# Sharing the first row scaling of a second RMS norm between VectorE and ScalarE, and moving the wait for the sub-keys, in a one-core Trainium2 decoder block

## The chip, the cores and the metric

The kernel runs on one core of one Trainium2 chip. A core has the engines TensorE (PE in the profile, its weight loads PEld), VectorE (DVE), ScalarE (ACT), GpSimd (POOL) and SyncE (SP, which issues the DMAs here). The metric is the device time of one execution in microseconds (us), lower is better. The kernel before takes 3376.47 us, the median of 3 runs (3375.99 to 3376.52).

## The reference, cut to what matters

One layer of a hybrid decoder trunk over 16 meta tokens and 512 real tokens of width 2048:

```python
h = h + concat([att, rec]) @ w_out          # attention and a recurrent mixer
h = h[:, N_META:]                            # 512 tokens x 2048
h = h + peer_ffn(rms_norm(h, ln_ffn_g), peer_w_q, peer_sub_keys, peer_u, peer_v)
```

The change lies at the start of the second line's work. `rms_norm` divides each token's row by the root of its mean square and multiplies by a gain per column. `peer_ffn` then multiplies the normed rows by `w_q` (8 heads x 256 columns), splits each head's query into two halves, scores each half against 128 sub-keys, and picks the 16 best experts out of 128 x 128 by the two halves' top 16. All products are in float32, kept accurate by splitting both operands into a high and a low part and adding three products.

## The kernel before, in words

Everything is one program of successive stages, each with its own block of instructions per engine: `project`, `attend`, `recur`, `mix_out` (the product with `w_out`), `route` (second norm, query product, scores, top 16), `gate_table`, `experts`. An engine's instructions run in the order in which they are written; between engines there are only semaphores (a wait stands ahead of an instruction, an increment behind one). `route` starts at about 920 us of the trace and ends at about 1175 us, `experts` runs from about 1325 us to the end.

Tokens lie as four tiles of 128 rows (`TB` = 4), the 2048 columns as 16 columns of 128 (`DC` = 16). At the start of `route`:

- VectorE finishes the statistics and the inverse root (`inverse_root`, lines 104 to 108), then `scale_row` (line 1863) multiplies h by it, tile by tile and half a row (1024 columns) at a time, into `scaled_rows`. The four first halves stand ahead of everything; the four second halves stand between the first four `low_column` instructions.
- TensorE keeps itself busy with three products on the identity, then `turn_x` (line 1611) transposes the scaled rows, 4 transposes (one for each tile) per column, into one of four PSUM banks. The first four columns are turned ahead of the first product, later ones one per column of the first head.
- ScalarE's `high_column` (line 1688) takes a turned column out of PSUM, times the gain, as the high part; VectorE's `low_column` (line 1868) makes the low part.
- TensorE's `head(0, ...)` multiplies column by column: 6 matmuls (3 products for 2 query halves), each column after its `x_low`. Ahead of head 0 stands `pe.wait_ge(keys_loaded, 16)`: the sub-keys, a load of 1 MB that SyncE issues at the start of `route` (line 2614, behind the 1 MB load of the gain row). They are first used in `scores(1, ...)` (line 1622), after the first quarter of head 1's product, which scores head 0.
- GpSimd's `plain` (line 2622) waits for all eight half rows, multiplies the last tile by the gain row, and SyncE stores it (line 2617) ahead of the loads of `w_q` for head 1. Behind `plain` GpSimd makes the low parts of `w_q` (`split_low`, line 179).

The order around the change is written out by hand; there is no planner.

```python
            stay_busy_with(pe, q_bank[1][1][:, :].rearrange("p (b t) -> p b t", t=P), cst["ident"], 3)
            for c in range(len(turn_banks)):
                turn_x(c)
            pe.wait_ge(keys_loaded, 16)
            each_head(pe, head, 4)
```

Of the kernel before, what the change touches and what calls it, by code (L numbers as in the profile page):

```python
# [25 lines left out]
ACT = mybir.ActivationFunctionType  # L26
# [7 lines left out]
D = 2048  # L34
DC = D // P
T = 512
TB = T // P
# [1462 lines left out]
def early_step(key, half):  # L1500

    return PH + key // 2, key % 2 * 2 + half
# [7 lines left out]
NORM_HALVES = 2  # L1510


def route(nc, place, kb, stream, h, scaled_rows, sums, xT, picks, cst, load_keys, keys_loaded, plain, plain_stored,
# [3 lines left out]
    with ExitStack() as ctx:  # L1517
        def sem(name):
            return ctx.enter_context(nc.semaphore(f"route_{name}"))
# [15 lines left out]
        stat = place("route_norm_stat", [P, 4, TB], F32, kb)  # L1535
        x_hi, x_lo = xT
        gain = cst["ln_ffn"]
        meaned, rooted, scaled = sem("meaned"), sem("rooted"), sem("scaled")
        x_turned, x_high, x_low = sem("x_turned"), sem("x_high"), sem("x_low")

        q_done, q_out, s_done, s_out = sem("q_done"), sem("q_out"), sem("s_done"), sem("s_out")
# [18 lines left out]
        @block.sync  # L1560
        def _(sp):
            load_keys(sp)
            stream.load_rest(sp, PH)
            for key in range(EARLY + LATER // 2):
                for half in range(2):
                    load_early_half(sp, stream, u, key, half)

        @block.gpsimd
        def _(pool):
            def weigh(m, s, cs=range(2)):  # L1570

                if 0 in cs:
                    pool.wait_ge(places_met, m - 1)
                for c in cs:
                    last = pool.tensor_tensor(
                        hot[:, s, c], hot[:, s, c],
                        idx_f[:, s, c].unsqueeze(2).to_broadcast([P, TB, TOPK, TOPK]), ALU.mult)
                if 1 in cs:
                    last.then_inc(hot_done, 1)

            def head(m, s, first):
                for g in range(QSTEPS):
                    if not (first and m == 0 and g < 2):
                        stream.split_low(pool, m, g)
                    if g == 1 and not first:
                        weigh(m, s)

            plain(pool, scaled, NORM_HALVES * TB)
            each_head(pool, head, 2)
            stream.split_low_in_pieces(pool, *early_step(0, 0))  # L1590
            stream.split_low_in_pieces(pool, *early_step(0, 1))
            stream.split_low_in_pieces(pool, *early_step(1, 0))
            weigh(PH, 0, [0])
            stream.split_low_in_pieces(pool, *early_step(1, 1))
            weigh(PH, 0, [1])
            stream.split_low_in_pieces(pool, *early_step(2, 0))
            stream.split_low_in_pieces(pool, *early_step(2, 1))
            stream.split_low_in_pieces(pool, *early_step(3, 0))
            stream.split_low_in_pieces(pool, *early_step(3, 1))
            stream.split_low_in_pieces(pool, *early_step(EARLY, 0))  # L1600

        @block.tensor
        def _(pe):
            stream.start_free(pe)

            def turn_x(c):
                if c >= len(turn_banks):
                    pe.wait_ge(x_low, c - len(turn_banks) + 1)
                for tb in range(TB):
                    pe.wait_ge(scaled, c // (DC // NORM_HALVES) * TB + (tb + 1))  # L1610
                    last = pe.transpose(turn_banks[c % len(turn_banks)][:, tb, :],
                                        scaled_rows[:, tb, c * P:(c + 1) * P], cst["ident"][:, :])
                last.then_inc(x_turned, 1)

            def scores(m, s, wait_bank=True):

                for k in range(2):
                    pe.wait_ge(q_out, m * 2 + (k - 1))
                    if wait_bank:
                        pe.wait_ge(s_out, m * 2 + (k - 5))  # L1620
                    for tb in range(TB):
                        last = pe.matmul(s_bank[s][k][:, tb, :], qT[:, k, tb * P:(tb + 1) * P],
                                         cst["sub_keys"][:, m * 2 + (k - 2), :],
                                         start=True, stop=True)
                    last.then_inc(s_done, 1)
# [42 lines left out]
            stay_busy_with(pe, q_bank[1][1][:, :].rearrange("p (b t) -> p b t", t=P), cst["ident"], 3)  # L1668
            for c in range(len(turn_banks)):
                turn_x(c)  # L1670
            pe.wait_ge(keys_loaded, 16)
            each_head(pe, head, 4)
            for key in range(EARLY):
                early_key(key)
# [2 lines left out]
        def _(act):  # L1677
# [13 lines left out]
            def split_rows():  # L1691
                act.wait_ge(meaned, 1)
                act.activation(stat[:, 2], stat[:, 1], ACT.Sqrt).then_inc(rooted, 1)
                for c in range(DC):
                    high_column(c)
                    if c % QSPAN == QSPAN - 1 and c >= 2 * QSPAN - 1:
                        stream.split_high(act, *divmod(c // QSPAN + 1, QSTEPS))
# [45 lines left out]
        def _(dve):  # L1743
# [128 lines left out]
            dve.tensor_scalar(stat[:, 1], stat[:, 0], 1.0 / D, EPS, ALU.mult, ALU.add).then_inc(meaned, 1)  # L1872
            dve.wait_ge(rooted, 1)
            inverse_root(dve, link, *(stat[:, k] for k in (3, 1, 2, 0)))
            for tb in range(TB):
                scale_row(0, tb)
            for c in range(DC):
                if c < TB:
# [846 lines left out]
```

## Time and profile before

| | |
|---|---|
| median of 3 runs | 3376.47 us (3375.99 to 3376.52) |
| the profiled execution's own time | 3382.86 us |
| its span, first to last instruction | 3380.8 us |
| PE busy | 3301.9 us (98% of the span) |
| DVE busy | 2184.1 us (65%) |
| ACT busy | 1115.2 us (33%) |
| POOL busy | 1184.8 us (35%) |
| mean granted clock of TensorE | 0.996 |

The span is that of the one profiled execution, which took 6.39 us longer than the median of the runs. Busy shares are averages over stages with different limits. A start in the timeline is in us from the span's first instruction, a row with a count (x5) covers instructions that follow each other, and what stands in brackets is the idle time ahead of it and what ended it. Matmuls overlap, so the busy time of single ones adds up to more than the time they take together.

### The profile page before, as it was taken

The page shows a single profiled execution, that of the slowest core. Times are in us where ns is not written, and L with a number is a line of the kernel's source. Part 1 is how long each engine was busy: PE and PEld are TensorE (multiplying, and loading weights), DVE is VectorE, ACT ScalarE, POOL GpSimd, SP SyncE. Part 2 cuts the span into 40 slices and gives each one's busy share as a digit, 9 for nine tenths or more (in the row PEclk, how much of TensorE's full clock was granted, in tenths as well). Part 3 has the DMA queues.
Part 4 walks back from the last instruction along what each step waited for, and adds up shares of the span by engine and source line. Part 5 has one row for each costly group of instructions (what it writes and reads, how often), then busy time and mean ns, then how long its engine had stood idle before and what let it go on. Part 6 is the DMA issues. An engine that isn't in the chain of part 4 may idle for free.

```text
span 3380.8 us, 49648 instructions
## 1 busy us (share of the span) xinstructions
PE 3301.9 (98%) x16960; PEld 2897.7 (86%) x16960; DVE 2184.1 (65%) x3841; ACT 1115.2 (33%) x1746; POOL 1184.8 (35%) x914
## 2 busy tenths in 40 slices
PE   8999999999999889999999999999999999999999
PEld 6778877878787788889989998999899899989988
DVE  2003413881168898787877677777777777777776
ACT  3122223652232397332222223222222223222321
POOL 3344431454345501243433223322333333333332
PEclk9999999999999999999999999999999999999999
DMA  4233330004332256888888888888888888888886
GB/s 151 81 89 97 94 87 26 26 26 143 105 100 83 93 201 233 270 288 302 300 297 272 267 265 262 274 265 267 262 270 266 264 271 264 265 262 271 267 263 233
DMA packets 369233, 686.52 MB, mean 203 GB/s; under 512 B 212816, under 2 KB 213200, under 8 KB 365904
## 3 DMA queue, kind: packets, MB, share of 16 engines
q1 hardware_dynamic: 295408, 416.79, 39.0%
q0 software_dynamic: 73728, 268.47, 23.2%
q8 instruction: 57, 0.93, 0.1%
q14 instruction: 40, 0.33, 0.0%
HBM read 654.76 MB, written 30.41 MB: 203 GB/s over the span
## 4 chain that ended last, share of the span: by engine, by line
PE 61%; DVE 0%; issue 0%
PE shared L2273 10%; PE shared L2271 10%; PE shared L2272 10%; PE exp_o L2295 7%; PE exp_o L2297 7%; PE exp_o L2293 7%; PE shared L2293 3%; PE shared L2295 3%; PE shared L2297 3%; PE exp_o L241 0%; DVE h L2418 0%
## 5 line engine op out<-in xcount | busy, mean ns | idle before, releaser
L2273 PE MATMUL shared<-x_high,exp_ul 128*128 128x384 f32 x1920 | 641.7, 334 | 0.0
L2271 PE MATMUL shared<-x_high,exp_uh 128*128 128x384 f32 x1920 | 641.6, 334 | 0.0
L2272 PE MATMUL shared<-x_low,exp_uh 128*128 128x384 f32 x1920 | 641.5, 334 | 0.0
L2252 POOL DMA_INDIRECT exp_rows<-in_v_rows,exp_now x256 | 327.6, 1280 | 709.7 <-DVE h L2409 658.2
L2252 POOL DMA_INDIRECT exp_rows<-in_u_rows,exp_now x256 | 301.3, 1177 | 651.4 <-DVE exp_rows L2402 591.5
L2331 ACT CAST exp_vh<-exp_raw 128x1024 fp32r<-128x1024 f32 x252 | 256.0, 1051 | 502.0 <-PE exp_o L2297 292.5
L2388 DVE TENSOR_TENSOR exp_vl<-exp_raw,exp_vh 128x1024 fp32r<-128x1024 f32 x256 | 304.6, 1221 | 148.6 <-ACT exp_vh L2331 148.2
L2293 PE MATMUL exp_o<-exp_vh,exp_ah 128*128 128x512 f32 x1024 | 398.5, 389 | 1.3 <-issue 1.3
L2297 PE MATMUL exp_o<-exp_vh,exp_al 128*128 128x512 f32 x1024 | 399.0, 390 | 0.0
L2295 PE MATMUL exp_o<-exp_vl,exp_ah 128*128 128x512 f32 x1024 | 398.9, 390 | 0.0
L2350 ACT ACTIVATE exp_act<-shared 128x384 f32<-128x384 f32 x120 | 59.1, 492 | 921.5 <-PE shared L2273 921.5
L2271 PEld LDWEIGHTS shared<-x_high,exp_uh 128*128 128x128 f32 x1920 | 360.5, 188 | 1.2
L2272 PEld LDWEIGHTS shared<-x_low,exp_uh 128*128 128x128 f32 x1920 | 360.5, 188 | 1.2
L2273 PEld LDWEIGHTS shared<-x_high,exp_ul 128*128 128x128 f32 x1920 | 360.5, 188 | 0.0
L179 POOL TENSOR_TENSOR w_in_lo<-w_in_raw,w_in_hi 128x1024 fp32r<-128x1024 f32 x88 | 213.7, 2429 | 327.6 <-ACT w_in_hi L162 312.5
L2409 DVE SCALAR_TENSOR_TENSOR h<-exp_rows,exp_weights,h 128x1024 f32<-128x1024 f32 x256 | 316.6, 1277 | 0.0
L2388 DVE TENSOR_TENSOR exp_ul<-exp_raw,exp_uh 128x1024 fp32r<-128x1024 f32 x240 | 290.4, 1221 | 30.1 <-ACT exp_uh L2331 30.1
L2402 DVE SCALAR_TENSOR_TENSOR exp_rows<-exp_rows,sparse_x 128x1024 f32<-128x1024 f32 x256 | 302.8, 1218 | 8.6 <-DMA exp_rows<-in_u_rows,exp_now 8.4
L2443 DVE TENSOR_TENSOR exp_act<-exp_act,exp_gates 128x384 f32<-128x384 f32 x120 | 67.5, 563 | 314.6 <-ACT exp_act L2350 314.6
L2331 ACT CAST exp_uh<-exp_raw 128x1024 fp32r<-128x1024 f32 x240 | 248.7, 1049 | 0.0
L2293 PEld LDWEIGHTS exp_o<-exp_vh,exp_ah 128*128 128x128 f32 x1024 | 192.2, 188 | 41.6 <-issue 1.7
L2297 PEld LDWEIGHTS exp_o<-exp_vh,exp_al 128*128 128x128 f32 x1024 | 192.2, 188 | 40.1
(356 smaller groups left out, 6162.3 us busy)
## 6 DMA issues: line engine op xcount, KB each, us to landing
exp_raw<-in_v SPq DMA_DIRECT2D x256, 512.0 KB, 4.5
exp_raw<-in_u SPq DMA_DIRECT2D x240, 512.0 KB, 5.6
w_in_raw<-in_w_in SPq DMA_DIRECT2D x88, 512.0 KB, 3.7
gate_table<-table_stage SPq DMA_DIRECT2D x12, 2048.0 KB, 6.6
exp_gates<-gate_table SPq DMA_DIRECT2D x124, 192.0 KB, 6.4
w_out_raw<-in_w_out SPq DMA_DIRECT2D x32, 512.0 KB, 3.8
w_q_raw<-in_w_q SPq DMA_DIRECT2D x32, 512.0 KB, 3.8
w_q_raw<-in_u SPq DMA_DIRECT2D x16, 512.0 KB, 3.7
```

Of the source, the lines that this page charges most:

```text
L179: eng.tensor_tensor(self.lo[:, g % 2], self.raw[:, g % RAW], self.hi[:, g % 2].bitcast(F32), ALU.subtract).then_inc(self.low, 1)
L2252: pool.indirect_dma_start(rows[slot][:, :], None, sparse["v" if kind == "mix" else "u"], bass.IndirectOffsetOnAxis(ap=now[:, turn, place_n ...
L2271: pe.matmul(bank, uh[:, b, c, :], xh[:, 0:DENSE_TB, c, :], start=(c == 0), stop=False)
L2272: pe.matmul(bank, uh[:, b, c, :], xl[:, 0:DENSE_TB, c, :], start=False, stop=False)
L2273: last = pe.matmul(bank, ul[:, b, c, :], xh[:, 0:DENSE_TB, c, :], start=False, stop=(c == DC - 1))
L2293: pe.matmul(bank[:, :], ah[:, key, tokens], vh[:, dc % 2, key, :], start=(key == 0), stop=False)
L2295: pe.matmul(bank[:, :], ah[:, key, tokens], vl[:, dc % 2, key, :], start=False, stop=False)
L2297: last = pe.matmul(bank[:, :], al[:, key, tokens], vh[:, dc % 2, key, :], start=False, stop=(key == KEYS_OF_MACRO - 1))
L2331: act.copy(part(uh if kind == "u" else vh, kind, which, half), raw[:, c % RAW_SLOTS, :])\
L2388: dve.tensor_tensor(part(ul if kind == "u" else vl, kind, which, half), raw[:, slot, :], part(uh if kind == "u" else vh, kind, which, half ...
L2402: done = dve.scalar_tensor_tensor(rows[slot][:, :], rows[slot][:, :], 1.0, sparse["x"][:, half, :], ALU.mult, ALU.mult, accum_out=dots[:, ...
L2409: done = dve.scalar_tensor_tensor(sums, rows[slot][:, :], weights[:, pl(pick(m, kind, t), 1)], sums, ALU.mult, ALU.add)
```

## The change

ScalarE scales the first halves of tiles 1 and 3, behind a new semaphore `inverted` that VectorE raises after the inverse root, and reports them by a new semaphore `scaled_too`; VectorE keeps tiles 0 and 2. The transposes and `plain` wait for the two semaphores accordingly. TensorE's wait for the sub-keys moves from ahead of head 0 to the first `scores`.

```diff
-        meaned, rooted, scaled = sem("meaned"), sem("rooted"), sem("scaled")
+        meaned, rooted, scaled, scaled_too = sem("meaned"), sem("rooted"), sem("scaled"), sem("scaled_too")
+        inverted = sem("inverted")
...
-            plain(pool, scaled, NORM_HALVES * TB)
+            pool.wait_ge(scaled_too, TB // 2)
+            plain(pool, scaled, TB // 2 + TB)
...
                 for tb in range(TB):
-                    pe.wait_ge(scaled, c // (DC // NORM_HALVES) * TB + (tb + 1))
+                    if c < DC // NORM_HALVES:
+                        pe.wait_ge(scaled_too if tb % 2 else scaled, tb // 2 + 1)
+                    else:
+                        pe.wait_ge(scaled, TB // 2 + (tb + 1))
...
             def scores(m, s, wait_bank=True):
 
+                if isinstance(m, int) and m == 1:
+                    pe.wait_ge(keys_loaded, 16)
                 for k in range(2):
...
             for c in range(len(turn_banks)):
                 turn_x(c)
-            pe.wait_ge(keys_loaded, 16)
             each_head(pe, head, 4)
...
                 act.activation(stat[:, 2], stat[:, 1], ACT.Sqrt).then_inc(rooted, 1)
+                act.wait_ge(inverted, 1)
+                for tb in range(1, TB, 2):
+                    act.activation(scaled_rows[:, tb, 0:D // NORM_HALVES], h[:, tb, 0:D // NORM_HALVES],
+                                   ACT.Copy, scale=stat[:, 3, tb:tb + 1]).then_inc(scaled_too, 1)
                 for c in range(DC):
                     high_column(c)
...
             inverse_root(dve, link, *(stat[:, k] for k in (3, 1, 2, 0)))
-            for tb in range(TB):
+            dve.sem_inc(inverted, 1)
+            for tb in range(0, TB, 2):
                 scale_row(0, tb)
```

On VectorE at the start of `route` (L108 ends the inverse root, `scaled_rows` are the scaled rows, `x_low` the low columns), before:

```order
L108 TENSOR_TENSOR route_norm_stat<-route_norm_stat 128x4 [waits route_chain]
L1863 TENSOR_SCALAR scaled_rows<-h,route_norm_stat 128x1024 [waits route_chain]
L1863 TENSOR_SCALAR scaled_rows<-h,route_norm_stat 128x1024 x4
L1868 SCALAR_TENSOR_TENSOR x_low<-route_s,c_ln_ffn,x_high 128x4x128 [waits route_x_high]
L1863 TENSOR_SCALAR scaled_rows<-h,route_norm_stat 128x1024
L1868 SCALAR_TENSOR_TENSOR x_low<-route_s,c_ln_ffn,x_high 128x4x128 [waits route_x_high]
```

and now:

```order
L108 TENSOR_TENSOR route_norm_stat<-route_norm_stat 128x4 [waits route_chain]
L1873 TENSOR_SCALAR scaled_rows<-h,route_norm_stat 128x1024 [waits route_chain]
L1873 TENSOR_SCALAR scaled_rows<-h,route_norm_stat 128x1024 x2
L1878 SCALAR_TENSOR_TENSOR x_low<-route_s,c_ln_ffn,x_high 128x4x128 [waits route_x_high]
L1873 TENSOR_SCALAR scaled_rows<-h,route_norm_stat 128x1024
L1878 SCALAR_TENSOR_TENSOR x_low<-route_s,c_ln_ffn,x_high 128x4x128 [waits route_x_high]
```

Three half rows (two first halves, one second half) stand ahead of the first low column where five stood. On ScalarE the two others stand between the square root (L1699, which was L1693) and the high columns, with no other instruction added:

```order
L1699 ACTIVATE route_norm_stat<-route_norm_stat 128x4 [waits route_meaned]
L1702 ACTIVATE scaled_rows<-h,route_norm_stat 128x1024 [waits route_inverted]
L1702 ACTIVATE scaled_rows<-h,route_norm_stat 128x1024
L1694 ACTIVATE x_high<-route_s,c_ln_ffn 128x4x128 [waits route_x_turned] x8
L162 CAST w_q_hi<-w_q_raw 128x1024 [waits w_q_used,w_q_loaded2]
```

On TensorE the first product of head 0 (into `route_q`, behind the transposes into `route_s`) stood so before:

```order
L1611 MATMUL route_s<-c_ident,scaled_rows 128x128 [waits route_scaled] x16
L231 MATMUL route_q<-x_high,w_q_hi 128x512 [waits route_x_low,w_q_low,sub_keys_loaded]
L232 MATMUL route_q<-x_high,w_q_lo 128x512
L233 MATMUL route_q<-x_low,w_q_hi 128x512
L231 MATMUL route_q<-x_high,w_q_hi 128x512
```

and the first product and the first scores stand so now:

```order
L1616 MATMUL route_s<-c_ident,scaled_rows 128x128 [waits route_scaled]
L1616 MATMUL route_s<-c_ident,scaled_rows 128x128 [waits route_scaled_too]
L231 MATMUL route_q<-x_high,w_q_hi 128x512 [waits route_x_low,w_q_low]
L232 MATMUL route_q<-x_high,w_q_lo 128x512
...
L233 MATMUL route_q<-x_low,w_q_hi 128x512
L1629 MATMUL route_s<-sub_keys,route_qT 128x128 [waits route_q_out,sub_keys_loaded]
L1629 MATMUL route_s<-sub_keys,route_qT 128x128 x3
```

The wait for the sub-keys has gone from the first product to the first score, one head later; the transposes wait for the two semaphores by turns.

## Rows read from the trace of the kernel before

**Rows 1.** Stretches of the span: busy us of each engine, then clock, DMA share, GB/s.

```profile
core 0: us, PE busy (x) PEld busy (x) DVE busy (x) ACT busy (x) POOL busy (x), PEclk, DMA share, GB/s
920.00:927.20 7.20, 5.22 (x22) 2.88 (x22) 6.24 (x15) 2.62 (x5) 0.00 (x0) 1.00 0.69 291
927.20:970.00 42.80, 42.80 (x220) 35.82 (x221) 18.73 (x62) 16.36 (x22) 17.81 (x7) 1.00 0.33 111
970.00:1130.00 160.00, 152.93 (x710) 126.25 (x709) 140.19 (x724) 39.38 (x50) 89.69 (x41) 0.99 0.26 83
1175.00:1325.00 150.00, 136.31 (x982) 121.32 (x983) 140.93 (x447) 140.36 (x345) 9.17 (x12) 0.99 0.48 194
1325.00:3380.80 2055.80, 2047.43 (x10373) 1864.42 (x10371) 1540.38 (x1902) 593.62 (x748) 669.04 (x580) 1.00 0.83 271
```

**Rows 2.** Timeline of TensorE around the first product: transposes (L1611), products.

```profile
924.35 1.40 PEld L1611 LDWEIGHTS route_s<-c_ident,scaled_rows 128*128 128x128 f32 x13 [0.52 <-DVE scaled_rows L1863]
924.35 1.64 PE L1611 MATMUL route_s<-c_ident,scaled_rows 128*128 128x128 f32 x13 [0.33 <-DVE scaled_rows L1863]
927.20 0.50 PE L231 MATMUL route_q<-x_high,w_q_hi 128*128 128x512 f32 x1 [1.22 <-DMA sub_keys<-in_sub_keys]
929.05 0.48 PE L231 MATMUL route_q<-x_high,w_q_hi 128*128 128x512 f32 x1
```

**Rows 3.** Timeline of VectorE there: inverse root, row scalings, low columns.

```profile
920.10 0.17 DVE L1872 TENSOR_SCALAR route_norm_stat<-route_norm_stat 128x4 f32<-128x4 f32 x1
...
921.35 0.16 DVE L108 TENSOR_TENSOR route_norm_stat<-route_norm_stat 128x4 f32<-128x4 f32 x1
921.55 3.40 DVE L1863 TENSOR_SCALAR scaled_rows<-h,route_norm_stat 128x1024 f32<-128x1024 f32 x5
925.43 0.75 DVE L1868 SCALAR_TENSOR_TENSOR x_low<-route_s,c_ln_ffn,x_high 128x512 fp32r<-128x512 f32 x1 [0.48 <-ACT x_high L1688]
926.10 0.74 DVE L1863 TENSOR_SCALAR scaled_rows<-h,route_norm_stat 128x1024 f32<-128x1024 f32 x1
926.76 0.74 DVE L1868 SCALAR_TENSOR_TENSOR x_low<-route_s,c_ln_ffn,x_high 128x512 fp32r<-128x512 f32 x1
```

**Rows 4.** Timeline of ScalarE there: square root, high columns; a cast pair before.

```profile
907.71 2.00 ACT L167 CAST w_q_hi<-w_q_raw 128x1024 fp32r<-128x1024 f32 x2
...
920.31 0.20 ACT L1693 ACTIVATE route_norm_stat<-route_norm_stat 128x4 f32<-128x4 f32 x1 [0.71 <-DVE route_norm_stat L1872]
924.71 2.42 ACT L1688 ACTIVATE x_high<-route_s,c_ln_ffn 128x512 fp32r<-128x512 f32 x4 [4.20 <-PE route_s L1611]
```

**Rows 5.** Groups of ScalarE by form: count, busy us, mean ns, idle before.

```profile
L162 ACT CAST w_q_hi<-w_q_raw 128x1024 fp32r<-128x1024 f32 x46 | 48.1, 1045 | 121.5 <-PE route_q L233 103.8 <-PE route_q L1663 17.8
L1688 ACT ACTIVATE x_high<-route_s,c_ln_ffn 128x512 fp32r<-128x512 f32 x16 | 10.7, 688 | 17.0 <-PE route_s L1611 17.0
L1711 ACT COPY route_qT<-route_q 128x512 f32<-128x512 f32 x8 | 4.7, 587 | 28.5 <-PE route_q L233 28.5
```

**Rows 6.** Timeline of VectorE at its first top 16 (semaphore steps are not shown).

```profile
962.85 1.65 DVE L1758 MAX8 route_val<-route_scores 128x8 f32<-128x128 f32 x8 [11.96 <-ACT route_scores L1684]
...
973.28 0.23 DVE L1828 CAST route_idx_f<-route_idx 128x128 f32<-128x128 uint32 x1 [0.24 <-DVE route_idx L1762]
```

**Rows 7.** Timelines of ScalarE, GpSimd, SyncE: next work behind the change.

```profile
935.39 1.04 ACT L162 CAST w_q_hi<-w_q_raw 128x1024 fp32r<-128x1024 f32 x1
...
929.64 4.61 POOL L2622 TENSOR_TENSOR plain_rows<-scaled_rows,ln_ffn_row 128x2048 f32<-128x2048 f32 x1 [14.65 <-DVE scaled_rows L1863]
936.51 2.40 POOL L179 TENSOR_TENSOR w_q_lo<-w_q_raw,w_q_hi 128x1024 fp32r<-128x1024 f32 x1 [2.27 <-ACT w_q_hi L162]
...
920.23 0.43 SPq L2614 DMA_DIRECT2D sub_keys<-in_sub_keys  x1
```

**Rows 8.** Waits from 970 to 1000 us: engine, line, what ended it, us, times.

```profile
PE route_q L231 <- POOL w_q_lo L179: 1.9, 1, 1.9
```

**Rows 9.** Stretches after that wait, columns as in rows 1.

```profile
992.50:995.00 2.50, 2.00 (x7) 1.62 (x8) 2.21 (x13) 0.00 (x0) 2.50 (x2) 0.87 0.37 80
995.00:997.50 2.50, 2.50 (x7) 1.98 (x6) 2.25 (x16) 0.00 (x0) 0.29 (x1) 0.50 0.66 218
997.50:1000.00 2.50, 2.50 (x12) 1.99 (x12) 2.21 (x15) 0.00 (x0) 0.00 (x0) 0.95 0.31 121
```

**Rows 10.** Waits from 1000 to 1050 us, columns as in rows 8.

```profile
PE route_q L231 <- POOL w_q_lo L179: 2.1, 2, 1.3
```

## The prediction

> **What bounds the kernel now.** I first read the busy time by stretches of the span. The largest part, from 1325 us to the end, has TensorE busy for 2047 of 2056 us [rows 1]: nothing before it makes it shorter, it can only start earlier. The same holds one stage back, where VectorE and ScalarE are each busy for about 140 of 150 us [rows 1]. So the question is by how much `route` hands over sooner. In `route` the product of head 0 runs from 927.20 us with no gap of TensorE up to 970 us (42.80 busy of 42.80) [rows 1], while VectorE waits 11.96 us for the first scores, until 962.85 us [rows 6]. Whatever brings the first product forward therefore brings the first scores forward by as much, as long as none of its feeders becomes late.
>
> Then I read the timelines of the three engines up to the first product. The reader is to see two waits in a row. The first: the transposes wait for the fourth row scaling. VectorE's five scalings start at 921.55 us and take 3.40 us together, one 0.75 us by the later rows [rows 3], so a new one starts every (3.40 - 0.75) / 4 = 0.66 us, and the fourth ends at 921.55 + 3 x 0.66 + 0.75 = 924.28 us. The weight load of its transpose starts at 924.35 us [rows 2], 0.07 us later. From there the chain runs: high column at 924.71 us [rows 4], which takes 0.69 us [rows 5]; low column at 925.43 us, done at 926.18 us [rows 3]. The second: the first product needs only that low column, but starts at 927.20 us, and what ended its wait is the DMA of the sub-keys [rows 2], issued at 920.23 us [rows 7]. TensorE stands idle for 1.22 us there [rows 2].
>
> **The change part by part.** *The sub-keys.* Without that wait the first product would start behind the low column, at 926.18 us plus 0.07 us as between scaling and transpose, so at 926.25 us. That is worth 927.20 - 926.25 = 0.95 us. The wait itself moves to the first scores; these need head 0's queries, and the top 16 on them begins at 962.85 us [rows 6], some 30 us after the sub-keys are there, so it costs nothing. Nothing is queued behind a wait that is already met.
>
> *VectorE's increment.* `inverted` is an instruction of its own ahead of the scalings. The trace shows no such step; the nearest row is the cast in the top 16, with two increments and a wait for its own result ahead of it, that stands idle for 0.24 us [rows 6], against 0.04 us with the wait alone (921.51 to 921.55 us) [rows 3]. So one costs 0.10 us (0 to 0.20). VectorE's and ScalarE's first scalings start at about 921.65 us: ScalarE's square root starts 0.04 us behind the VectorE step it waits for (920.27 to 920.31 us) [rows 3, 4].
>
> *ScalarE's two half rows.* No row shows this form. The nearest by size is the cast of 128x1024, 1.05 us [rows 5], of which a pair takes 2.00 us [rows 4], 0.95 us from start to start. The nearest by form is the high column with its scale per partition, 0.69 us against 0.59 us for a plain copy of the same size [rows 5], so 0.10 us for the scale. I take 1.15 us for one and 1.05 us from start to start: tiles 1 and 3 end at 922.80 and 923.85 us. At the bounds (no surcharge, no increment: 923.55 us; no overlap of the pair and 0.20 us for the increment: 924.05 us) the last first half comes 0.73 to 0.23 us before the 924.28 us of now; I take 924.28 - 923.85 = 0.43 us. VectorE ends tile 2 at 921.65 + 0.66 + 0.75 = 923.06 us, so ScalarE sets the end, and its high columns, at 924.28 us, are not held up. No table load is among ScalarE's instructions there, before or now, and the copies behind the square root needed none.
>
> The Trainium skill speaks against this part: "ScalarE: Activation LUTs", section "Rules for kernel authors", gives plain multiplications to VectorE and not to ScalarE. Instruction for instruction the trace agrees, 1.15 against 0.75 us; by that rule this part would bring nothing and the sum would be the sub-keys' part alone.
>
> *Behind the first product.* With both parts it starts at 927.20 - 0.95 - 0.43 = 925.82 us, before the sub-keys. A column takes 1.85 us (927.20 to 929.05 us) [rows 2]; low columns follow each other at 1.33 us with a scaling between them (925.43 to 926.76 us) [rows 3], so they stay ahead. The three scalings ahead of the first low column end at 923.7 us, before its high column does (924.97 us). `plain` on GpSimd moves forward with the scalings, by some 0.4 us: from 929.64 to 929.2 us, done at 933.8 us [rows 7]. The next low part of `w_q` waits for ScalarE's cast, now at 935.39 us and then at 934.0 us, so it starts at 935.1 us instead of 936.51 us [rows 7], and `plain` is out of the way. The loads for head 1 wait for the store of `plain`, which moves by 0.4 us only; they have 12 us and more until head 1.
>
> *Sum*: 0.95 + 0.43 = 1.38 us, between 0.23 us (if the sub-keys' part were nothing) and 1.68 us. In the profiled execution that makes 3382.86 - 1.38 = 3381.48 us (span 3379.4 us). The median of the runs is 6.39 us below the profiled execution, and where these lie is not known; the difference carries over: 3376.47 - 1.38 = **3375.1 us**. That is 0.04%, far less than 0.2% (6.75 us), about what a measurement of this kernel can tell from no change.
>
> **The rivals.**
>
> *The ScalarE share brings nothing.* If its two activations take as long as the four scalings, or start late, only the 0.95 us of the sub-keys stays: 3375.5 us. It needs 0.43 us more than I put in, beyond my bounds; against it stand the rows for cast and scale, for it only that no row shows the form. The Trainium skill's rule named above ("ScalarE: Activation LUTs", "Rules for kernel authors") is this case.
>
> *The sub-keys are not late, so half of the change does nothing.* Landing is fixed by the DMA, and the runs without a profile are 6.39 us shorter; if they land 1 us earlier there, only the 0.43 us stay: 3376.0 us. Against it stands that the row names this DMA outright.
>
> *A further fall of the clock, and the kernel gets slower.* At the first wait of TensorE for the low parts of `w_q`, 1.9 us long [rows 8], the granted clock falls: 0.87, 0.50 and 0.95 in three stretches of 2.5 us [rows 9], so that (0.13 + 0.50 + 0.05) x 2.5 / 0.5 = 3.4 us run at 1.2 instead of 2.4 GHz and 1.7 us are lost. The next two such waits, 2.1 us together and at most 1.3 us [rows 10], bring no fall. If the new timing lets one more of these waits bring a fall, the gain of 1.38 turns into a loss of 0.3 us: 3376.8 us. It decides from one fall on, wherever it comes. Against it: the work from the first scores on moves as a whole, so the waits keep their lengths.
>
> *The fall at 995 us goes away*: 1.38 + 1.7 us, 3373.4 us. The same reason speaks against it.
>
> **How the numbers follow.** Both parts pay: 0.62, with a range of its own of 3374.6 to 3375.6 us. ScalarE share nothing: 0.12. Sub-keys not late, or the gain lost further back: 0.09. Further fall: 0.09. Fall gone: 0.08. All of these lie between 3373.4 and 3376.8 us, and I give 3373.3 to 3377.0 us. Faster by over 0.2% would take 5 us that no row offers: 0.01. Slower by over 0.2% would take five further falls of 1.7 us: 0.02. Within 0.2%: 0.97.
>
> **What would show it.** In the new profile, VectorE's first scalings should be a group of three from about 921.65 us, with two activations of about 1.15 us on ScalarE beside them; the first high column at about 924.3 us; the first product at about 925.8 us, its wait ended by the low column and not by a DMA; no idle time of TensorE from there to the first scores, and the top 16 at about 961.5 us. I am wrong if an activation takes over 1.4 us, if TensorE waits for a second low column or for `w_q`, or if the first scores come earlier and the end does not.

## The result and the profile after

The changed kernel takes **3387.19 us** (median of 7 runs, 3384.29 to 3388.96). The kernel before took 3376.47 us in 7 runs beside it, 3372.91 to 3379.48. That is a ratio of 1.003, 95% interval 1.0019 to 1.0041: slower by 10.7 us, where 3375.1 us was forecast and the range ended at 3377.0 us. The profiled execution took 3387.55 us, its span is 3385.5 us.

Both parts of the change do what they were meant to. Timelines of the kernel after at the start of `route`, the rows that answer to [rows 2 to 4, 6, 7], of TensorE, VectorE, ScalarE and GpSimd:

```profile
923.98 1.64 PE L1616 MATMUL route_s<-c_ident,scaled_rows 128*128 128x128 f32 x13 [0.38 <-ACT scaled_rows L1702]
925.96 0.47 PE L231 MATMUL route_q<-x_high,w_q_hi 128*128 128x512 f32 x1 [0.34 <-DVE x_low L1878]
...
921.48 0.16 DVE L108 TENSOR_TENSOR route_norm_stat<-route_norm_stat 128x4 f32<-128x4 f32 x1
921.79 2.08 DVE L1873 TENSOR_SCALAR scaled_rows<-h,route_norm_stat 128x1024 f32<-128x1024 f32 x3 [0.15 <-DVE route_norm_stat L108]
925.06 0.75 DVE L1878 SCALAR_TENSOR_TENSOR x_low<-route_s,c_ln_ffn,x_high 128x512 fp32r<-128x512 f32 x1 [1.19 <-ACT x_high L1694]
961.57 0.68 DVE L1768 MAX8 route_val<-route_scores 128x8 f32<-128x128 f32 x3 [11.94 <-ACT route_scores L1690]
...
921.74 2.19 ACT L1702 ACTIVATE scaled_rows<-h,route_norm_stat 128x1024 f32<-128x1024 f32 x2 [1.10 <-DVEq L1885]
924.34 1.84 ACT L1694 ACTIVATE x_high<-route_s,c_ln_ffn 128x512 fp32r<-128x512 f32 x3 [0.42 <-PE route_s L1616]
...
929.29 4.61 POOL L2633 TENSOR_TENSOR plain_rows<-scaled_rows,ln_ffn_row 128x2048 f32<-128x2048 f32 x1 [14.18 <-DVE scaled_rows L1873]
935.25 2.41 POOL L179 TENSOR_TENSOR w_q_lo<-w_q_raw,w_q_hi 128x1024 fp32r<-128x1024 f32 x1 [1.35 <-ACT w_q_hi L162]
```

The transposes are now released by ScalarE, the first product by the low column instead of the sub-keys, at 925.96 instead of 927.20 us. `route` itself began 0.13 us later in this execution (the inverse root's last step at 921.48 against 921.35 us [rows 3]), so the gain is 1.37 us at the first product (1.38 forecast). At the first top 16 it is 1.41 us (961.57 against 962.85 us [rows 6]). Both are against the one profile that the prediction was made from. In a second profile of the kernel before (below) the sub-keys land earlier: its first product starts 6.32 us after the reciprocal of the inverse root instead of 6.66 us, and 5.29 us in the change, so against that one the gain is 1.03 us.

The time is lost behind that. Stretches of the kernel after, columns as in [rows 1]:

```profile
927.20:970.00 42.80, 42.80 (x222) 35.84 (x221) 19.50 (x68) 16.38 (x22) 19.00 (x7) 1.00 0.33 111
970.00:1130.00 160.00, 148.37 (x678) 122.29 (x677) 142.50 (x684) 38.02 (x48) 85.51 (x36) 0.97 0.25 81
1175.00:1325.00 150.00, 135.06 (x977) 122.51 (x976) 141.56 (x447) 137.71 (x340) 11.16 (x15) 0.98 0.47 191
1325.00:3385.50 2060.50, 2051.67 (x10396) 1867.95 (x10396) 1541.28 (x1906) 596.66 (x754) 670.09 (x581) 1.00 0.83 271
```

Up to 970 us TensorE still has no gap. From 970 to 1130 us, the middle heads, it is busy for 148.37 us where it was 152.93 [rows 1], at a clock of 0.97 for 0.99. `experts` has only moved: 2056.5 to 2056.6 us from its first product to the end of the span in every kernel here.

What TensorE waits for there, from the view of the waits between 1000 and 1180 us (engine, line, what ended it, us, times, longest). After:

```profile
PE route_q L231 <- POOL w_q_lo L179: 9.7, 5, 3.8
```

and before:

```profile
PE route_q L231 <- POOL w_q_lo L179: 5.2, 5, 1.3
```

The same five waits for GpSimd's low part of `w_q`, but 4.5 us longer together, and two of them are long (3.77 and 3.51 us). **The race behind the first long one** is in the timelines of head 3. (From here on heads are counted from 1 by VectorE's work: head 3 is VectorE's `head(2, ...)`, while GpSimd and TensorE are already at `head(4, ...)`.) Kernel after, VectorE (one stall, then its last small operations on positions, `route_pos_f`), GpSimd, TensorE:

```profile
1025.05 0.26 DVE L1775 MATCH_REPLACE8 route_cand_rest<-route_best,route_cand 128x112 f32<-128x112 f32 x1
1025.80 0.81 DVE L1768 MAX8 route_best<-route_cand_rest 128x8 f32<-128x112 f32 x4 [0.50 <-DVE route_cand_rest L1775]
1029.04 0.23 DVE L1818 SCALAR_TENSOR_TENSOR route_pos_f<-route_quarterf 128x64 f32<-128x64 f32 x1
1029.30 2.42 DVE L1820 SCALAR_TENSOR_TENSOR route_pos_f<-route_pos_f,route_quarterf 128x64 f32<-128x64 f32 x1
1034.50 2.36 DVE L1827 TENSOR_TENSOR route_hot<-route_pos_f,c_iota 128x1024 f32<-128x1024 f32 x2
...
1029.24 2.40 POOL L179 TENSOR_TENSOR w_q_lo<-w_q_raw,w_q_hi 128x1024 fp32r<-128x1024 f32 x1 [3.47 <-ACT w_q_hi L162]
1036.94 4.74 POOL L1576 TENSOR_TENSOR route_hot<-route_hot,route_idx_f 128x1024 f32<-128x1024 f32 x2 [5.30 <-DVE route_hot L1827]
1041.63 4.69 POOL L179 TENSOR_TENSOR w_q_lo<-w_q_raw,w_q_hi 128x1024 fp32r<-128x1024 f32 x2
...
1044.04 0.50 PE L231 MATMUL route_q<-x_high,w_q_hi 128*128 128x512 f32 x1 [3.77 <-POOL w_q_lo L179]
```

and before:

```profile
1031.86 0.22 DVE L1810 SCALAR_TENSOR_TENSOR route_pos_f<-route_pos_f,route_quarterf 128x64 f32<-128x64 f32 x1
1032.12 0.22 DVE L1812 TENSOR_TENSOR route_pos_f<-route_pos_f,route_quarterf 128x64 f32<-128x64 f32 x1
...
1032.14 2.48 POOL L179 TENSOR_TENSOR w_q_lo<-w_q_raw,w_q_hi 128x1024 fp32r<-128x1024 f32 x1 [3.17 <-ACT w_q_hi L162]
1037.31 4.74 POOL L1575 TENSOR_TENSOR route_hot<-route_hot,route_idx_f 128x1024 f32<-128x1024 f32 x2 [2.69 <-DVE route_hot L1817]
...
1044.43 0.50 PE L231 MATMUL route_q<-x_high,w_q_hi 128*128 128x512 f32 x1 [1.26 <-POOL w_q_lo L179]
```

Before, VectorE's last small operation starts 0.02 us ahead of GpSimd's low part and takes 0.22 us. After, GpSimd starts 0.06 us ahead of the last but one, and that operation takes 2.42 us, until GpSimd is done. GpSimd's own multiplication (`weigh`) needs VectorE's result: it begins 7.70 us after the start of that low part (1029.24 to 1036.94) where it was 5.17 us, the next low parts stand behind it, and TensorE waits 3.77 for 1.26 us, so 2.51 us longer. It happens again in head 5. VectorE, GpSimd, TensorE there:

```profile
1083.27 2.35 DVE L1822 TENSOR_TENSOR route_pos_f<-route_pos_f,route_quarterf 128x64 f32<-128x64 f32 x1
...
1083.14 2.39 POOL L179 TENSOR_TENSOR w_q_lo<-w_q_raw,w_q_hi 128x1024 fp32r<-128x1024 f32 x1 [3.48 <-ACT w_q_hi L162]
...
1097.68 0.80 PE L231 MATMUL route_q<-x_high,w_q_hi 128*128 128x512 f32 x1 [3.51 <-POOL w_q_lo L179]
```

With each long wait the clock falls; stretches of the kernel after, around the end of the second:

```profile
1095.00:1097.50 2.50, 0.00 (x0) 0.00 (x0) 2.35 (x16) 0.31 (x1) 2.50 (x2) 0.78 0.00 0
1097.50:1100.00 2.50, 2.32 (x6) 1.84 (x7) 2.35 (x17) 0.00 (x0) 2.45 (x2) 0.50 0.46 133
1100.00:1102.50 2.50, 2.50 (x7) 1.97 (x6) 2.12 (x12) 0.00 (x0) 0.00 (x0) 0.50 0.69 203
1102.50:1105.00 2.50, 2.50 (x11) 2.02 (x10) 2.21 (x18) 0.00 (x0) 0.00 (x0) 0.85 0.21 84
```

Half speed, 1.2 GHz. In the first of these stretches TensorE does nothing, so its fall costs nothing; the other three lose 0.50 x 2.32 + 0.50 x 2.50 + 0.15 x 2.50 = 2.8 us. Behind the first long wait the clock is 0.54 and 0.77 in the two stretches from 1045 to 1050 us, so (0.46 + 0.23) x 2.5 = 1.7 us. Together: 4.5 us of longer waits and 4.5 us of slower clock, 9.0 us.

So the question for the experiments: why does VectorE lose a race that it won by 0.02 us, when all before it came 1.4 us earlier? I had three theories. One: the **rhythm** of the heads depends on when head 0 starts, or on the fall of the clock at 993 us [rows 9], which the profile of after lacks. Two: **ScalarE's** two scalings themselves disturb something. Three: **VectorE's instruction stream**. Its program is one instruction shorter (two scalings less, one increment more), and the trace of after has two stalls that before has not: ahead of the `MAX8` above VectorE stands idle for 0.50 us (1025.05 + 0.26 = 1025.31 to 1025.80 us), elsewhere 0.15 us. In the trace's list of VectorE's instructions it is number 1161 of the span (counted from 0, semaphore and register steps among them). The other, of the same size, is number 1033, 128 instructions earlier, at 1001.01 us. If something costs VectorE some 0.35 us at every 128th instruction, mostly under running work, the shift by one lays it bare behind a wait.

### The profile page after: what moved, and what is told of

It reads as the page before. It is cut to its first block, busy times and chain, and to the rows that moved or that the text cites. A ratio compares the mean times of both kernels' runs of the same rounds, so it can differ in the third digit from the quotient of the medians.

```text
span 3385.5 us, 49650 instructions
## 1 busy us (share of the span) xinstructions
PE 3305.2 (98%) x16960; PEld 2903.5 (86%) x16960; DVE 2187.3 (65%) x3839; ACT 1117.4 (33%) x1748; POOL 1184.6 (35%) x914
## 4 chain that ended last, share of the span: by engine, by line
PE 60%; DVE 0%; issue 0%
PE shared L2284 10%; PE shared L2282 10%; PE shared L2283 10%; PE exp_o L2306 7%; PE exp_o L2308 7%; PE exp_o L2304 7%; PE shared L2306 3%; PE shared L2304 3%; PE shared L2308 3%; PE exp_o L241 0%; DVE h L2429 0%
## 5 line engine op out<-in xcount | busy, mean ns | idle before, releaser
L2342 ACT CAST exp_vh<-exp_raw 128x1024 fp32r<-128x1024 f32 x252 | 255.8, 1051 | 502.7 <-PE exp_o L2308 292.8
```

The lines of the kernel that those rows point to most:

```text
L2342: act.copy(part(uh if kind == "u" else vh, kind, which, half), raw[:, c % RAW_SLOTS, :])\
```

## The experiments

Each time is a median with its range; the ratio is against the kernel before on the same chip (its median there was 3380.38 us for the first four kernels of the table, 3376.85 us for the next four and 3375.71 us for the last two), with its 95% interval.

| kernel | us (range, runs) | ratio (interval) |
|---|---|---|
| before, unchanged | 3374.88 (3373.44 to 3382.10, 10) | 0.999 (0.998 to 0.9999) |
| sub-keys alone | 3375.75 (3373.02 to 3383.08, 10) | 0.9996 (0.9986 to 1.0005) |
| ScalarE's share alone | 3388.15 (3385.61 to 3391.23, 9) | 1.0025 (1.0015 to 1.0035) |
| change, head 0 delayed | 3393.33 (3392.96 to 3396.32, 4) | 1.0045 (1.0028 to 1.0062) |
| change, 1 increment more | 3375.61 (3374.99 to 3378.08, 11) | 0.9996 (0.9987 to 1.0005) |
| before, 23 increments more | 3388.02 (3384.01 to 3392.06, 8) | 1.0033 (1.0023 to 1.0043) |
| before, 4 increments more | 3376.98 (3373.29 to 3380.75, 10) | 0.9999 (0.999 to 1.0009) |
| change, later multiplication | 3375.02 (3373.64 to 3378.12, 10) | 0.9994 (0.9984 to 1.0003) |
| before, later multiplication | 3377.73 (3376.87 to 3380.12, 11) | 1.0005 (0.9996 to 1.0014) |
| change, later, 1 increment more | 3376.69 (3373.70 to 3378.45, 11) | 0.9999 (0.999 to 1.0008) |

The first row is the kernel before against itself, and its interval just misses 1: a tenth of a per cent is not to be trusted here. Single runs of one kernel lie up to 10 us apart; the profiles show falls of the clock at differing places (from some 1130 us on most of all), but what all of that scatter is was not settled.

**Before, unchanged.**

> The kernel before, unchanged, for a second profiled execution. Theory A (rhythm): the loop of heads falls into one of two rhythms, and which one follows from where TensorE's early wait of 1.9 us for the low parts of w_q brings a fall of the clock; then an execution without a fall near 993 us must show waits of TensorE of 3 us and more in every second head and end some 5 to 10 us later, one with the fall heads of 24.7 to 25.1 us. Theory B (the change itself slows the loop): heads as in the first profile whatever the clock does. Time 3373 to 3380 us by both.

Its profile has no fall of the clock in the heads at all, although its first wait for the low part is 1.9 us too, and its heads are as short as the others' of before (24.7 to 25.2 us from one copy of the queries to the next, from the third on; in the change two of them take 29.2 and 30.0 us, the others 24.7 us). So the fall in [rows 9] was no lasting part of the kernel, and a rhythm that hangs on it falls.

**The sub-keys alone.**

```diff
             def scores(m, s, wait_bank=True):
+                if isinstance(m, int) and m == 1:
+                    pe.wait_ge(keys_loaded, 16)
...
-            pe.wait_ge(keys_loaded, 16)
             each_head(pe, head, 4)
```

> Only the wait for the sub-keys is moved, VectorE scales all rows. The first product starts at about 926.3 us, the first scores come some 0.9 us earlier. Theory A: the end is either some 1 us earlier (3375.5 us) or in the slow rhythm (3383 to 3389 us), nothing between. Theory B with the sub-keys' wait as the cause: 3386 to 3388 us; with ScalarE's share as the cause: 3375.5 us.

3375.75 us. In the profile the first product's wait is ended by the low column, as forecast. VectorE's stream is untouched, the last small operation starts at 1026.75, GpSimd's low part at 1026.76 us. This half is harmless.

**ScalarE's share alone**, which is the rest of the change's diff.

> Only the scaling is shared with ScalarE, the wait for the sub-keys stands ahead of head 0 as before. The first product then starts where the sub-keys land, at 927.2 us, so the first scores come no earlier. Theory A: as before, 3373 to 3380 us. Theory B with ScalarE's share as the cause: 3386 to 3388 us; with the sub-keys' wait: 3376 us.

3388.15 us: all of the loss is in this half, and its first product, at 924.91 us, comes 6.47 us after the reciprocal of the inverse root, between the 6.32 and 6.66 us of the two profiles of before. An earlier start is not the cause. VectorE and GpSimd in its timelines:

```profile
1024.84 0.81 DVE L1767 MAX8 route_best<-route_cand_rest 128x8 f32<-128x112 f32 x4 [0.50 <-DVE route_cand_rest L1774]
1028.34 2.40 DVE L1819 SCALAR_TENSOR_TENSOR route_pos_f<-route_pos_f,route_quarterf 128x64 f32<-128x64 f32 x1
...
1028.26 2.40 POOL L179 TENSOR_TENSOR w_q_lo<-w_q_raw,w_q_hi 128x1024 fp32r<-128x1024 f32 x1 [3.46 <-ACT w_q_hi L162]
```

The same stall, the same race lost, by 0.08 us.

**The change, with head 0 delayed** by eight products on the identity.

```diff
             for c in range(len(turn_banks)):
                 turn_x(c)
+            stay_busy_with(pe, q_bank[1][1][:, :].rearrange("p (b t) -> p b t", t=P), cst["ident"], 8)
             each_head(pe, head, 4)
```

> The change as it is, with eight products on the identity (8 x 0.23 = 1.8 us) on TensorE between the transposes and head 0, so that the first product starts at about 927.4 us, as before the change, with all its new instructions and waits in place. Theory A: back to before, 3374 to 3380 us. Theory B: the slow loop stays, 3386 us and more.

The delay came out far larger than the 1.8 us that I had meant: the eight products are 16 matmuls and take 7.03 us. TensorE's timeline there:

```profile
927.00 7.03 PE L241 MATMUL route_q<-c_ident 128*128 128x512 f32 x16
933.47 0.79 PE L231 MATMUL route_q<-x_high,w_q_hi 128*128 128x512 f32 x1
```

So the experiment doesn't put the start back to that of before: the first product comes 11.25 us after the reciprocal, where it was 6.66 us before and 5.29 us in the change. It still speaks: head 0 starts 6.0 us later than in the change, the time of 3393.33 us is 6.1 us longer than the change's, and the operation at 1037.16 us takes 2.42 us beside a low part that began at 1037.10 us. So a later start of head 0 does not mend the loop. Between ScalarE's instructions and VectorE's stream the next three decide; all add empty semaphore increments to VectorE where it is about to stand idle for 12 us.

**The change, one increment more.** VectorE's stream has the length of before again, and ScalarE still scales.

```diff
                 low_column(c)
+            for _ in range(1):
+                take_wait()
             dve.wait_ge(plain_stored, 16)
```

> The change with one more semaphore increment on VectorE, in its idle time between the last low column and the first top 16, so that every later VectorE instruction stands at the place in the stream that it had before the change. Theory C (place in the stream): the change leaves VectorE one instruction shorter; thereby a hiccup of 0.35 us at every 128th instruction shows behind two waits in the first pass of the loop (gaps of 0.45 us at the 1033rd and 1161st), and in head 3 VectorE comes 0.33 us later and loses a race against GpSimd's low part of w_q (an operation of 0.23 us takes 2.42 us). With the one instruction back both gaps go, no operation of VectorE takes 2.4 us in heads 3 to 6, TensorE waits 1.3 us at most in heads 3 to 6, and the time is 3374 to 3378 us, about 1.4 us below the kernel before. Theory D (ScalarE's two scalings, or the semaphores, slow the loop by themselves): 3385 to 3389 us, as the change.

3375.61 us: one instruction that does nothing gives the 11 us back. VectorE and GpSimd:

```profile
1024.64 0.26 DVE L1775 MATCH_REPLACE8 route_cand_rest<-route_best,route_cand 128x112 f32<-128x112 f32 x1
1025.05 0.81 DVE L1768 MAX8 route_best<-route_cand_rest 128x8 f32<-128x112 f32 x4
1028.80 0.22 DVE L1822 TENSOR_TENSOR route_pos_f<-route_pos_f,route_quarterf 128x64 f32<-128x64 f32 x1
...
1028.86 2.43 POOL L179 TENSOR_TENSOR w_q_lo<-w_q_raw,w_q_hi 128x1024 fp32r<-128x1024 f32 x1 [3.48 <-ACT w_q_hi L162]
1033.98 4.78 POOL L1576 TENSOR_TENSOR route_hot<-route_hot,route_idx_f 128x1024 f32<-128x1024 f32 x2 [2.70 <-DVE route_hot L1827]
```

The `MAX8` now starts 0.15 us after the step before it ends (1024.90 to 1025.05 us), and VectorE wins by 0.06 us. Compare with the change: from the `MAX8` to the low part's start it was 3.44 us (1025.80 to 1029.24), here 3.81 us. VectorE has 0.37 us more.

**Before, 23 increments more**, at the same place. The shift was chosen so that a 128th instruction falls behind a wait of head 3 again, with ScalarE not involved.

> The kernel before, with nothing of the change, and 23 semaphore increments on VectorE in its idle time of 12 us ahead of the first top 16. This shifts its stream so that only the second crossing, in head 3, falls right behind a wait (and not the first, in head 2). Theory C: one gap of about 0.45 us in head 3, VectorE 0.3 us later there, the race lost, waits of TensorE of 3.5 us and more in every second head, and 3384 to 3390 us with none of the change in it. Theory D: as before, 3374 to 3382 us.

3388.02 us: the kernel before, made slow by increments alone.

```profile
970.97 0.23 DVE L1828 CAST route_idx_f<-route_idx 128x128 f32<-128x128 uint32 x1 [0.63 <-DVE route_idx L1762]
...
1023.34 0.81 DVE L1758 MAX8 route_best<-route_cand 128x8 f32<-128x112 f32 x4 [0.50 <-DVE route_cand L1791]
1029.99 2.42 DVE L1810 SCALAR_TENSOR_TENSOR route_pos_f<-route_pos_f,route_quarterf 128x64 f32<-128x64 f32 x1
...
1029.93 2.40 POOL L179 TENSOR_TENSOR w_q_lo<-w_q_raw,w_q_hi 128x1024 fp32r<-128x1024 f32 x1 [3.18 <-ACT w_q_hi L162]
```

The stalls stand at other instructions of the program now, but at numbers 905 and 1161 of the stream, two times 128 apart. The cast's 0.63 us stand against 0.24 us before [rows 6].

**Before, 4 increments more.** Here a 128th instruction falls behind a wait in head 2 only.

> The kernel before with 4 such increments: only the first crossing, in head 2, falls right behind a wait. VectorE then waits for head 2's scores anyway (1.7 us), so the gap of 0.35 us is taken up there. Theory C: a gap in head 2 and none in head 3, the race in head 3 won as before, 3374 to 3382 us. If it is slow, the shift as such does it, not the second gap. Theory D: as before.

3376.98 us, as before. VectorE in heads 2 and 3, then GpSimd:

```profile
998.87 0.81 DVE L1758 MAX8 route_best<-route_cand_rest 128x8 f32<-128x112 f32 x4 [0.50 <-DVE route_cand_rest L1765]
...
1028.05 0.23 DVE L1812 TENSOR_TENSOR route_pos_f<-route_pos_f,route_quarterf 128x64 f32<-128x64 f32 x1
...
1028.05 2.49 POOL L179 TENSOR_TENSOR w_q_lo<-w_q_raw,w_q_hi 128x1024 fp32r<-128x1024 f32 x1 [3.17 <-ACT w_q_hi L162]
```

The stall is there (number 1033), but it costs nothing: VectorE waits for the next scores anyway (1.73 us, until 1009.73 us). So it is not the number of increments that makes the loss, it is where the stall falls. Rhythm and ScalarE are out as theories; the stream stands.

**The change, with GpSimd's multiplication one quarter later.** This leaves the stalls: the third low part of a head no longer stands behind a multiplication that waits for VectorE.

```diff
-                    if g == 1 and not first:
+                    if g == 2 and not first:
                         weigh(m, s)
```

> The change (slow place in the stream kept) with one move on GpSimd: its multiplication of the last head's places stands behind the third low part of w_q in each head, not behind the second. Both theories say that TensorE's waits come from the third low part standing behind the multiplication, which waits for VectorE. If so, TensorE's waits of 0.8 to 3.8 us for the low parts go in heads 3 to 6 and with them the falls of the clock there, even if VectorE still loses races: 3370 to 3378 us. If TensorE only meets the same wait one step later: 3384 to 3390 us.

3375.02 us. Heads take 24.3 us, and no fall of the clock lies in them. The stall is still there, in front of the same `MAX8`; the last line is from the view of the waits from 1000 to 1130 us:

```profile
1024.50 0.81 DVE L1768 MAX8 route_best<-route_cand_rest 128x8 f32<-128x112 f32 x4 [0.50 <-DVE route_cand_rest L1775]
1028.26 0.23 DVE L1822 TENSOR_TENSOR route_pos_f<-route_pos_f,route_quarterf 128x64 f32<-128x64 f32 x1
...
1029.36 2.40 POOL L179 TENSOR_TENSOR w_q_lo<-w_q_raw,w_q_hi 128x1024 fp32r<-128x1024 f32 x1 [2.60 <-ACT w_q_hi L162]
...
PE route_q L231 <- POOL w_q_lo L179: 2.1, 5, 0.4
```

VectorE now has 1.1 us to spare instead of a few hundredths. So the edit does more than was meant: the race is no longer lost at all, and what the later multiplication does for TensorE while VectorE still loses was not seen.

**The kernel before, with the same edit**, and **the change with both mends.**

> The kernel before with GpSimd's multiplication of the picks one quarter later in the order (g == 2 for g == 1), nothing else. The kernel with the change and the same edit took 3375.02 us, ratio 0.9994. Theory (the change costs only where VectorE loses the race with GpSimd's low part; its own 1.38 us are real): heads of 24.3 us as there, waits of TensorE for w_q_lo of 0.4 us, no falls of the clock in the heads; 3374 to 3378 us, and at most 1.4 us above the changed kernel with the same edit, which is below what can be told. Rival (the later multiplication only helps where the race is lost): heads of 24.7 to 25.2 us and waits of 1 us and more for w_q_lo as in the kernel before.

> The change, with GpSimd's multiplication one quarter later and one empty increment on VectorE ahead of the wait for the stored rows. Each of the two edits by itself brings the time back to 3375 to 3376 us. Theory (one mechanism, both edits break it at different steps): nothing adds up; heads of 24.3 us, waits for w_q_lo of 0.4 us, 3374 to 3377 us. Rival (two separate losses, each mended by one of the edits): about 9 to 10 us less than either, near 3365 us.

3377.73 and 3376.69 us. Both mends together bring no more than either alone, where two separate losses would have given some 3365 us, so there is one loss and not two. The rival put against the theory for the kernel before falls as well: the later multiplication shortens the heads of the kernel before too, to 24.3 us with waits of 2.0 us together. No version beats the kernel before by more than the measurement can tell. Where these shorter heads go shows in this table, worked out from rows of each profile (the starts of the reciprocal at the start of `route`, of ScalarE's last copy of queries and of the first product of `experts`), one profiled execution each, in us:

| kernel | reciprocal to last copy | last copy to `experts` | sum |
|---|---|---|---|
| before (first profile) | 209.8 | 193.9 | 403.7 |
| before (second profile) | 207.9 | 196.3 | 404.1 |
| sub-keys alone | 207.3 | 191.6 | 398.9 |
| change, 1 increment more | 206.8 | 191.6 | 398.4 |
| change | 215.5 | 192.7 | 408.3 |
| before, later multiplication | 202.7 | 197.9 | 400.6 |
| change, later multiplication | 201.6 | 195.9 | 397.4 |
| change, later, 1 increment more | 201.5 | 195.9 | 397.4 |

The change's loss lies in the first column: 7.6 us against the second profile of before, 8.2 and 8.7 us against the next two rows, and 5.7 us against the first profile of before, which has a fall of its own [rows 9]. The later multiplication gains 5 us or more there, and in the second column, where VectorE and ScalarE are busy for about 140 of 150 us [rows 1], it gives back 4.3 us in the change (191.6 to 195.9 us) and 1.6 to 4.0 us in the kernel before. And with the race out of the way, something like the change's own gain appears: 202.7 - 201.6 = 1.1 us between two executions, too little for the medians to tell.

## Why the prediction was wrong

*The sub-keys (0.95 us): right in kind, large in size.* The wait is ended by the low column. Alone the move brings the first product to 5.79 us after the reciprocal, where it was 6.66 us in the first profile of before and 6.32 us in the second: 0.53 to 0.87 us. The DMA that the term was read from lands at differing times, and the prediction had one execution to go by.

*VectorE's increment (0.10 us): right as a duration*, 0.15 us from the inverse root to the scalings (921.64 to 921.79 us) for 0.04 us, so 0.11 us. *ScalarE's half rows (0.43 us): right.* Two in 2.19 us against 1.05 + 1.15 = 2.20 us forecast (the 1.15 us for one was an estimate; no row of before had it). The rule of the Trainium skill, "ScalarE: Activation LUTs", section "Rules for kernel authors", by which this part would bring nothing, did not hold at this place: slower per row, the two still ended earlier than VectorE's third and fourth.

*The sum of 1.38 us: right as far as it went*, 1.37 us at the first product and 1.41 us at the first scores against the first profile of before, 1.03 us and 1.07 us against the second. That it agrees to a hundredth is luck.

*The step that failed* is a sentence on which the small chance of a loss rested: "the work from the first scores on moves as a whole, so the waits keep their lengths". Up to head 3 it moved as a whole on TensorE, ScalarE and GpSimd, but not on VectorE. There the increment was costed by its time, and the one thing that mattered was its count: two scalings out and one increment in make the stream one instruction shorter for all that follows. That laid a stall of 0.35 us bare in head 3, where VectorE had 0.02 us to spare against GpSimd. The rows of that margin were in the trace of before and were not read, since VectorE's small operations looked harmless at 0.22 us.

*The rival "a further fall of the clock"* had the right kind of loss, and its condition ("if the new timing lets one more of these waits bring a fall") was met. Its price was mis-sized: 1.7 us for one fall behind waits of unchanged length, where two waits grew by 4.5 us together and the falls cost 1.7 and 2.8 us, so 9.0 us lost where 1.7 us was put in. (Where the race is won by one increment more, the two long heads are 25.1 and 25.0 us instead of 29.2 and 30.0 us: 9.1 us.) Less the 1.0 to 1.4 us gained at the start this makes 7.6 to 8.0 us of the 10.7 us between the medians; what the rest is stays open, with single runs that scatter by up to 10 us. I had no mechanism that would lengthen the waits, and so gave "slower" 0.02. The chances of the five cases also add up to 1.00 by themselves, which left no room for that 0.02 and the 0.01 for "faster". Its own last sign of being wrong came true: the first scores came earlier and the end did not.

The chain, with what supports each link: stall at a 128th instruction (moved at will by 1, 4 and 23 increments) - VectorE 0.35 us later in head 3 - GpSimd's low part starts first and holds VectorE's small operation for 2.4 us (in the change and the three others of 3388 us and more, and in no other kernel, at this place) - multiplication and next low part 2.5 us later (read from the timelines; moving the multiplication takes the waits away, but the lost race with them) - TensorE waits 3.5 to 3.8 us - the clock falls. Two things were not tried. The first is what exactly VectorE does at a 128th instruction. The second is why only every second head is hit. VectorE's loop repeats two heads, and on its second pass the same `MAX8` (number 1449) stands idle again, though for less, ahead of the second lost race:

```profile
1079.51 0.81 DVE L1768 MAX8 route_best<-route_cand_rest 128x8 f32<-128x112 f32 x4 [0.27 <-DVE route_cand_rest L1775]
```

That is 0.12 us over the usual 0.15 us, and the race is lost by 0.13 us (1083.14 to 1083.27 us). It fits, but no run separates it from the changed spacing of the heads.

## What to carry to other kernels

Count instructions as well as microseconds: where an engine's stream gets longer or shorter, everything behind it may meet its stalls at other places, and a pad of one empty instruction can show in one run whether that is the cause. Before calling the work behind an edit unchanged, look in its loop for pairs of instructions on VectorE and GpSimd that start within a few hundredths of each other, and for an engine that has a waiting instruction ahead of what TensorE needs. Give such a race room (here by putting GpSimd's multiplication one quarter later, which by itself brought no time) before tuning by single microseconds, since otherwise a good edit can measure as a bad one.

## What the runs showed of the hardware that I had not expected

In `route` VectorE stalled by some 0.35 us (0.50 for 0.15 us, once 0.63 for 0.24 us) at each 128th instruction of its program that followed a wait: at numbers 905, 1033 and 1161 of the list in six different programs, whatever instruction stood there. In the kernel before the wait itself stands at 1033 and 1161, and no stall shows. It is the place in the program that counts and not the number in the list. The loop's second pass adds 288 to the list: number 1545, again a multiple of 128 on, stands behind a wait in six profiles without a stall (0.15 us), while number 1833 (1545 + 288) has one of 0.50 us in the kernel before with 23 increments. The Trainium skill, "Runtime: NRT & Kernel Launch", section "Instruction fetch mechanics", says that instructions are fetched in blocks of 256 and that crossing a block's edge is mostly hidden. If this is that crossing, the distance here is 128, and once it is not hidden it decides over 10 us. The traces point that way: queue q14, of the kind "instruction" on the profile's page, moves packets of 8192 B, and in the change one starts 0.67 to 0.68 us behind each of numbers 1033, 1161 and 1289, none between 1051 and 1130 us, while the loop repeats, and the next at 1131.01 us, some 0.6 us behind number 1705 (1417 + 288). (One more, at 1016.62 us, stands behind none of these numbers.) That the stall is the wait for such a fetch was not shown: on the loop's second pass 0.12 us of it are left with no packet.

A VectorE operation of 128x64 with two inputs took 2.42 us instead of 0.23 us when GpSimd's low part had started 0.06 us ahead of it, and 0.22 us when it itself started 0.02 us ahead. The Trainium skill, "SBUF — State Buffer", section "Who interferes with whom", describes a port pair that the two engines share under an exclusive lock; the rows agree, in duration (until GpSimd's instruction of 2.40 us is done) and in that the first to start wins. When VectorE won by 0.02 us, GpSimd's instruction took 2.48 us.

TensorE's waits of 3.77 and 3.51 us came with a clock of 1.2 GHz (0.50 granted) and cost 1.7 and 2.8 us more; those of 0.8 to 1.3 us in the heads did not. A wait of 1.9 us, at 989 to 1000 us, was followed by a fall in the first profile of before [rows 9], and not in the second, nor in six other profiles that have it.
